# Three edits in one kernel: attention queries computed in full-width tiles, one more projection by seven products, and attention token sums moved from GpSimd to VectorE

## What is computed

```python
c_q = rms_norm(u_mla[..., :Q_LORA], q_g)
q = jnp.einsum('blr,rf->blf', c_q, w_uq).reshape(B, L, MLA_HEADS, QK_DIM)   # 384 -> 8 x 96
q = jnp.concatenate([q[..., :QK_NOPE], rope_axial(q[..., QK_NOPE:], *rot)], axis=-1)
k, v = mla_keys_values(u_mla, kv_g, w_ukv, rot)                             # 256 -> 8 x (64 + 64)
o = block_attention(q, jnp.concatenate([k, kc], axis=1), jnp.concatenate([v, vc], axis=1))
```

```python
cnv = silu(layer_norm(causal_depthwise_conv(a * sigmoid(g)), ln_g, ln_b))   # 31 taps, 1024 channels
merged = (g_attn * (attn @ w_o_attn) + g_rnn * (rnn @ w_o_rnn) + g_conv * (cnv @ w_o_conv))
h = h + merged @ w_out
h = h + (silu(f @ w_ffn_gate) * (f @ w_ffn_up)) @ w_ffn_down
```

## Time and profile before

| | us |
|---|---|
| time, median of 3 runs | 1744.97 |
| lowest and highest of the 3 | 1736.07, 1745.1 |
| the profiled execution's own time | 1739.31 |
| its span on the core | 1737.5 |
| TensorE busy in it | 1675.0 (96%) |
| VectorE busy | 1147.8 (66%) |
| ScalarE busy | 552.7 (32%) |
| GpSimd busy | 661.8 (38%) |

### The profile page before, as it was taken

The page is one execution under the profiler, slowest core; times in us unless marked ns, Lnnn a source line. Parts: engine busy times, 40 slices in busy tenths (PEclk is TensorE's granted clock), DMA queues, the critical chain, the costliest instruction groups (busy, mean ns, idle before and its releaser), DMA issues.

```text
span 1737.5 us, 35985 instructions
## 1 busy us (share of the span) xinstructions
PE 1675.0 (96%) x14722; PEld 1480.8 (85%) x14722; DVE 1147.8 (66%) x2044; ACT 552.7 (32%) x1244; POOL 661.8 (38%) x581
## 2 busy tenths in 40 slices
PE   6999988999999999999999999999999998999999
PEld 3777646888889888878989999989888888999999
DVE  5646155665368789787757664368788896676643
ACT  3232363443343453433330010233554304120100
POOL 1535003554035122115645554164123046445652
PEclk9999996999999999999999999999999999999999
DMA  9333100000443444324344444443343343444543
GB/s 371 137 112 115 65 1 2 5 4 5 182 160 122 146 146 146 122 101 142 124 143 173 168 164 158 164 146 128 120 169 127 137 145 107 162 170 170 170 158 110
DMA packets 53379, 225.71 MB, mean 130 GB/s; under 512 B 5088, under 2 KB 29024, under 8 KB 29280
## 3 DMA queue, kind: packets, MB, share of 16 engines
q1 hardware_dynamic: 53216, 223.40, 36.8%
HBM read 222.34 MB, written 1.05 MB: 129 GB/s over the span
## 4 chain that ended last, share of the span: by engine, by line
PE 87%; DVE 6%; ACT 3%; DMA 1%; issue 1%; DVEq 1%; POOL 0%; SPq 0%; ACTq 0%
PE PS L783 18%; PE PS L740 16%; PE PS L1048 15%; PE PS L1072 8%; PE PS L2531 5%; PE PS L2643 3%; PE PS L2060 2%; PE PS L2073 2%; DVE arena L1455 2%; DMA ring<-stream_dram 1%; PE PS L722 1%; PE PS L2736 1%; PE PS L900 1%; PE PS L863 1%; PE PS L1012 1%
## 5 line engine op out<-in xcount | busy, mean ns | idle before, releaser
L783 PE MATMUL PS<-arena,ring 128*128 128x272 f32 (+1 forms) x1664 | 390.0, 389 | 0.3 <-DVE arena L1683 0.3
L783 PEld LDWEIGHTS PS<-arena,ring 128*128 128x128 f32 x1664 | 311.7, 190 | 59.7 <-issue 6.1
L1455 DVE SCALAR_TENSOR_TENSOR arena<-arena,par 128x272 f32<-128x272 f32 (+1 forms) x480 | 259.5, 599 | 7.4 <-issue 0.9
L1895 POOL TENSOR_TENSOR arena<-ring 128x512 f32<-128x512 f32 x48 | 68.7, 1431 | 443.8 <-DMA ring<-stream_dram 353.9
L740 PE MATMUL PS<-arena,ring 128*128 128x136 f32 (+1 forms) x1536 | 202.0, 280 | 1.4 <-ACT arena L1158 1.4
L740 PEld LDWEIGHTS PS<-arena,ring 128*128 128x128 f32 x1536 | 192.7, 191 | 8.1 <-ACT arena L1158 1.7
L740 PE MATMUL PS<-arena 128*128 128x136 f32 (+1 forms) x1152 | 147.9, 280 | 4.5 <-ACT arena L1138 3.0
L1048 PE MATMUL PS<-arena 128*128 128x136 f32 (+1 forms) x1280 | 152.1, 277 | 0.0
L1048 PEld LDWEIGHTS PS<-arena 128*128 128x128 f32 x1280 | 148.7, 191 | 0.0
L740 PEld LDWEIGHTS PS<-arena 128*128 128x128 f32 x1152 | 140.0, 191 | 5.8 <-POOL arena L1895 1.7
L1048 PE MATMUL PS<-arena,ring 128*128 128x136 f32 (+1 forms) x960 | 116.1, 277 | 0.0
(11 more groups left out here) (417 smaller groups left out, 2966.3 us busy)
## 6 DMA issues: line engine op xcount, KB each, us to landing
ring<-stream_dram SPq DMA_DIRECT2D x185, 1024.0 KB, 4.9
ring<-stream_dram SPq DMA_DIRECT2D x32, 512.0 KB, 4.0
ring<-stream_dram SPq DMA_DIRECT2D x16, 384.0 KB, 3.8
arena<-x_dram SPq DMA_DIRECT2D x1, 2048.0 KB, 8.3
cst<-const_dram SPq DMA_DIRECT2D x1, 1080.0 KB, 7.0
out_dram<-H SPq DMA_DIRECT2D x4, 256.0 KB, 3.1
cst<-const_dram SPq DMA_DIRECT2D x1, 912.0 KB, 12.7
arena<-stream_dram SPq DMA_DIRECT2D x1, 512.0 KB, 11.1
```

Of the source, the lines that this page charges most:

```text
L783: last = mm(PS[:, 2 * (j % 2) + f, nw], w[:, k, P * f:P * f + P], src[:, k, nw], start=k == 0, stop=k == KD - 1)
L1455: stt(CVG[:, c, NQ], CVA[:, c, j + Q0:j + T2], dw_w[l][:, c, j:j + 1], CVG[:, c, NQ], ALU.mult, ALU.add)
L1895: g.tensor_tensor(to[:, 0], w21, w22, ALU.add).then_inc(L["summed"], 1)
```

## The change

1. **Queries.** The 24 matmuls of 96 columns become 18 of 128 columns. A weight tile then holds one head and a third, and a PSUM bank holds tile i of both halves of the heads. ScalarE takes the heads apart by nine copies of 32, 64 or 96 partitions. The rotation's swaps move behind the keys. They write four different groups of 32 partitions of one bank, VectorE multiplies all of it at once, and ScalarE carries the product to the partitions of the queries. The gate rows move into the attention loop, behind its fourth score.
2. **Step 12** joins `MIXED`. The turning of the values moves from ahead of step 13 into its middle.
3. **Attention token sums** move from GpSimd (step 38) to VectorE (step 35 in the first layer, 33 in the second).
4. **Convolution.** `CONV_STEPS` becomes a list for each layer with work moved earlier; layer norm starts at step 36 in the first layer and stays at 37 in the second. The squares and the silu are split in two halves of four tiles, with copies between them.
5. ScalarE's gains (`gain`) of the merge are done between the copies of the next step.

```diff
-CONV_SUM_J = 37
+CONV_SUM_J, ATT_SUM_J = (36, 37), (35, 33)
-MIXED = [*range(2, 8), 9, 11, 15, ...
+MIXED = [*range(2, 8), 9, 11, 12, 15, ...
-              19: 4, ... 25: 1, 26: 1, 27: 4, 28: 5, 29: 3, 30: 5, 31: 5, 32: 3, 33: 4, 34: 4, 35: 5, 36: 1}
+               19: 4, 20: 3, 21: 4, 22: 3, 23: 3, 24: 4, 25: 1, 26: 1, **late}
+              for late in ({27: 4, 28: 8, 29: 3, 30: 7, 31: 5, 32: 3, 33: 4, 34: 4, 35: 1},
+                           {27: 5, 28: 5, 29: 6, 30: 8, 31: 6, 32: 4, 33: 3, 34: 2})]
...
 (VectorE)
+                if j == ATT_SUM_J[l]:
+                    dve.wait_ge(L["o_kept"], B["o_kept"] + len(R))
+                    x = AT.rearrange("p (k e) t -> p k e t", e=2)
+                    token_sums(v, x[:, :, 0], x[:, :, 1], TATT, n0, n1).then_inc(L["att_halves"], 1)
 (GpSimd)
-                if j == OA_J:
-                    pool.wait_ge(L["o_kept"], B["o_kept"] + len(rounds(l)))
-                    front_halves(pairs(AT), TATT, n0, n1, L["att_halves"])
-                    back_halves(pairs(AT), TATT, n0, n1, L["att_halves"])
 (ScalarE, in a mixed step)
                     copy_a(j)
+                    if j == CONV_SUM_J[l] + 1:
+                        square(0)
+                    if j == CONV_SUM_J[l] + 4:
+                        conv_silu(1).then_inc(L["conv_out"], 1)
...
                     copy_g(j)
+                    if j == CONV_SUM_J[l] + 1:
+                        square(1).then_inc(L["conv_sq"], 1)
                     copy_c(j)
 (TensorE, MLA)
-            for h in range(8):
-                if h >= 4:
-                    pe.wait_ge(mq_kept, h - 3)
-                for k in range(3):
-                    w = weights(UQ + h // 4, 3, 384)
-                    last = mm(PS[0:96, h % 4, 0:TX], w[:, k, 96 * (h % 4):96 * (h % 4) + 96], REST[:, 4 + k, :], ...
+            for i in range(3):
+                for g in range(2):
+                    w = weights(UQ + g, 3, 384)
+                    for k in range(3):
+                        last = mm(PS[:, i, TX * g:TX * g + TX], w[:, k, P * i:P * i + P], REST[:, 4 + k, :], ...
+                last.then_inc(mq_made, 1)
...
+            for i in range(4):
+                last = mm(PS[32 * i:32 * i + 32, 4, :], perm32[64:96, :],
+                          QM[64:96, 2 * i:2 * i + 2, :].rearrange("p h t -> p (h t)"), start=True, stop=True)
+            last.then_inc(swap_made, 1)
 (VectorE, MLA)
+            tt(TURNED.rearrange("p (h t) -> p h t", h=2), PS[:, 4, :]..., over(msin, 2), ALU.mult).then_inc(lat_normed, 1)
+            tt(QM[r, :, :], QM[r, :, :], over(mcos[r], 8), ALU.mult)
+            dve.wait_ge(lat_root, 2)
+            tt(QM[r, :, :], QM[r, :, :], PM[r, :, :]..., ALU.add).then_inc(roped, 1)
```

More of the change, by code:

```diff
@@ L215, in build @@
         KR = USH[:, 0, :]
+        TURNED = cut(37120, 512)
         LSQ, LSK = cut(28928, 3, TX), cut(29696, 2, T1)
@@ L1261, in keep_gates, with square, conv_silu, gain @@
                       ).then_inc(L["ga_kept"], 1)
-            def gain(j):
-                for k in (2 * (j - WO_J), 2 * (j - WO_J) + 1):
+            def square(i):
+                act.wait_ge(L["conv_cent"], B["conv_cent"] + 1)
+                return a(CSQ[:, 4 * i:4 * i + 4, NQ], CVG[:, 4 * i:4 * i + 4, NQ], ACT.Square)
+            def conv_silu(i):
+                act.wait_ge(L["conv_normed"], B["conv_normed"] + 1)
+                for k in range(4 * i, 4 * i + 4):
+                    last = a(CVG[:, k, NQ], CVG[:, k, NQ], ACT.Silu, bias=q2l["ln_b"][:, k:k + 1],
+                             scale=q2l["ln_g"][:, k:k + 1])
+                return last
+            def gain(j, tiles=(0, 1)):
+                for k in (2 * (j - WO_J) + f for f in tiles):
                     act.wait_ge(L["mixed"], B["mixed"] + k + 1)
@@ L1280, in scalar_layers @@
                         keep_d(j - 1)
+                    if j >= WO_J + 2:
+                        gain(j - 2, (1,))
                 else:
@@ L2648, in _ @@
             pe.wait_ge(tile_kept, plain_made(27))
-            for i in range(KD):
-                last = mm(PS[:, 7, 2 * i:2 * i + 2], ROWSG[:, i // 2, P * (i % 2):P * (i % 2) + P], SEL, start=True, stop=True)
-            last.then_inc(gate_rows, 1)
             pe.wait_ge(lat_normed, 1)
@@ L2676, in _ @@
                     pe.wait_ge(mk_kept, h - 2)
+                else:
+                    pe.wait_ge(mq_kept, 2 + h // 2)
                 for k in range(2):
@@ L2704, in _ @@
                        start=True, stop=True).then_inc(ms_made, 1)
+                if i == 3:
+                    pe.wait_ge(vt_kept, 4)
+                    for f in range(KD):
+                        last = mm(PS[:, 7, 2 * f:2 * f + 2], ROWSG[:, f // 2, P * (f % 2):P * (f % 2) + P], SEL,
+                                  start=True, stop=True)
+                    last.then_inc(gate_rows, 1)
                 if i >= 3:
@@ L2879, in _, with keep_queries @@
                     a(MT1[:, 0, 0:TX], MT1[:, 0, 0:TX], ACT.Exp, scale=-0.5).then_inc(lat_root, 1)
-            for h in range(8):
-                act.wait_ge(mq_made, h + 1)
-                a(QM[0:96, h, :], PS[0:96, h % 4, 0:TX], ACT.Copy).then_inc(mq_kept, 1)
+            def keep_queries(i, to, of, first):
+                return a(QM[to, first::4, :], PS[of, i, :].rearrange("p (g t) -> p g t", g=2), ACT.Copy)
+            quad = [slice(32 * i, 32 * i + 32) for i in range(4)]
+            act.wait_ge(mq_made, 1)
+            keep_queries(0, slice(0, 96), slice(0, 96), 0)
+            keep_queries(0, quad[0], quad[3], 1).then_inc(mq_kept, 1)
+            act.wait_ge(mq_made, 2)
+            keep_queries(1, quad[1], quad[0], 1)
+            keep_queries(1, quad[2], quad[1], 1)
+            keep_queries(1, halves(0), halves(1), 2).then_inc(mq_kept, 1)
+            act.wait_ge(mq_made, 3)
+            keep_queries(2, quad[2], quad[0], 2)
+            keep_queries(2, quad[0], quad[1], 3)
+            keep_queries(2, quad[1], quad[2], 3)
+            keep_queries(2, quad[2], quad[3], 3).then_inc(mq_kept, 1)
             for h in range(8):
@@ L2885, in _ @@
                 a(KM[0:64, h, :], PS[halves(h % 2), h % 4, :], ACT.Copy).then_inc(mk_kept, 1)
+            act.wait_ge(lat_normed, 2)
+            for i in range(4):
+                last = a(PM[64:96, i, :], TURNED[quad[i], :], ACT.Copy)
+            last.then_inc(lat_root, 1)
             for t in range(4):
@@ L3119, in _ @@
             dve.wait_ge(swap_made, 2)
[L3120 to L3126 removed]
+            tt(TURNED.rearrange("p (h t) -> p h t", h=2), PS[:, 4, :].rearrange("p (h t) -> p h t", h=2), over(msin, 2),
+               ALU.mult).then_inc(lat_normed, 1)
+            tt(QM[r, :, :], QM[r, :, :], over(mcos[r], 8), ALU.mult)
+            dr()
+            dve.wait_ge(lat_root, 2)
+            tt(QM[r, :, :], QM[r, :, :], PM[r, :, :].rearrange("p i (h t) -> p (i h) t", h=2), ALU.add).then_inc(roped, 1)
             for i in range(17):
```

94 lines of the change are left out of this document (37 added, 57 removed).

## The result

The changed kernel took 1717.4 us, the median of 4 runs (1715.66 to 1720.2). The kernel before took 1744.57, the median of 4 (1736.07 to 1745.1). The ratio is 0.9857, 95% interval 0.9824 to 0.989. A second comparison, beside the experiments, gave 0.9885 (0.9865 to 0.9905), from 1717.92 against 1738.77. The medians are 27.2 us apart in the first comparison and 20.9 in the second, and the forecast of 1719 (1708 to 1731) held. The profiled execution's span went from 1737.5 to 1716.4, so 21.1 us less, where the sum said 20.05. All executions were in the same, fast state.

What follows compares the result with a forecast made beforehand. TensorE was taken to bound the kernel, at 87% of its chain of waits. Gains of 6.8, 2.35, 3.4 and 7.5 us sum to 20.05, from 1739.31 to 1719 us, range 1708 to 1731.

Steps and rivals of the forecast that it cites:

- Queries, 6.8 forecast: MLA part: hidden gate rows 1.95, full-width query tiles 2.6, earlier keys 2.4, less 0.2; gain 6.8 us, bounds 2.1 and 7.5.
- The choice between 0.9 and 3.6: MLA part: four swaps take 0.9 us if they overlap; the rival, swaps one after another, 3.6, total 1722, chance 0.12.
- Step 12, 2.35 forecast: Both layers: mixing step 12 saves 0.65 each, and step 13's waits of 0.65 and 0.40 go; gain 2.35 us.
- up to 1.6 a layer: Step 12: the cost in each layer if VectorE's lateness beside GpSimd's weight sums is not covered; costed at nothing.
- the cover: Around step 12: VectorE idles 2.41 us ahead, then waits for ScalarE's roots; nobody waits for it until mid step 13.
- eighth: Step 12: if GpSimd's four sums fully block VectorE, the loss is about an eighth more than the share taken.
- Layer one, 3.4 forecast: Layer one, convolution's norm: waits and slow matmuls of 5.4 us, less 2.0 kept back; gain 3.4, bounds 1 and 5.4.
- the 1.5 that I kept: Layer one: 1.5 us of waits expected to remain, for the halved silu and VectorE's token sums `TCNV`.
- Layer two, 7.5 forecast: Layer two: idleness and slow matmuls of 11.9 us, less 4.4 expected to remain; gain 7.5, bounds 3.5 and 10.
- the relief of 7.0: Layer two: VectorE comes 7.0 us earlier to the norm's first sum, more than the pause of 6.09 there.
- 2.8 for GpSimd's drag: Layer two: some 2.8 us by which GpSimd's token sums slowed VectorE's taps, saved by moving those sums to VectorE.
- 0.8 for the silu, 2.3 for `TCNV`: Layer two: waits expected to remain, 0.8 us for the silu and 2.3 for VectorE's convolution token sums.

Runs made afterwards that it cites:

- e4: Changed kernel with the four swaps writing one group of output partitions in four banks and the old VectorE rotation; ratio 0.989 to the kernel before.
- e9: Changed kernel with the gate rows ahead of the queries and the turn of the values ahead of step 13 again; ratio 0.9937 to the kernel before.
- e2: Kernel before with only step 12 mixed and the turn of the values moved inside step 13; ratio 0.9998 to the kernel before.
- e6: Changed kernel with the old convolution step lists in both layers and the norm at step 37 in both; ratio 0.9915 to the kernel before.
- e5: Changed kernel with the attention token sums back on GpSimd; median 1722.39 us, ratio 0.9897 to the kernel before.
- e7: Changed kernel with ScalarE's squares, silu and gains each in one piece, behind their step's copies; ratio 0.9875 to the kernel before.
- the repeat: The changed kernel run once more without any edit; 1717.92 us, ratio 0.9885 to the kernel before.

## Why the prediction was right, and where its steps were not

**Queries, 6.8 forecast, 6.6 measured.** Each row came as worked out: 8.05 for the queries (7.85), a wait of 0.6 for copies (0.7), 0.99 for the swaps (0.9). The choice between 0.9 and 3.6 rested on the earlier trace rows, and e4 shows that it hangs on the four output groups, not on the place. Gate rows: 1.78 by e9 (1.95).

**Step 12, 2.35 forecast, 1.1 + 1.3 measured** (e2: 1.46 and 1.29). Right in sum, and e9 shows that the wait which the step would have made without the moved turn, 3.46 and 2.96, was never priced: I had taken the 0.65 and 0.40 of the earlier trace rows for it, and the "up to 1.6 a layer" without the cover is 4.9 and 4.8. The "eighth" by which a full block would exceed my share doesn't come out of the rows either: at a share of 0.75 it is a third, which the cover holds as well. The cover chosen (3.67 and two products) was enough for either.

**Layer one, 3.4 forecast, 3.2 measured.** The pause of 2.56 and the slower stretch behind it went, and 1.48 + 0.61 + 0.32 came for the 1.5 that I kept. The reason that I gave, squares within step 37, isn't the only one that suffices: e6 keeps step 37 for the first sum and has no pause either. The token sums back on GpSimd (e5) change nothing in layer one, the old list with the later norm is 0.9 us better (e6), and squares, silu and gains unsplit are 1.2 better (e7). So none of the three is needed there as long as the other two stay. Which of them alone takes the pause away wasn't tried, and the cause in layer one stays open to that extent.

**Layer two, 7.5 forecast, 6.8 and in the repeat 8.0 measured.** The size is right, the reason only half, and that the errors evened out is luck. I made the relief of 7.0 of 6.0 less for VectorE to do, 1.8 of new lateness, and 2.8 for GpSimd's drag. The runs show both: with the new lists the place of the token sums is worth 6.2 (e5), with the new place the lists are worth 4.2 (e6). That 2.8 is the term that was mis-sized. I took half of the 5.7 us for GpSimd's token sums, but they are four of the six operations beside those taps, and with the new lists all eight operations would have stood beside twelve taps and cost 8.2. With the old lists the move takes the pause from 6.09 to 3.75 (e6; step 12 leaves it at 6.09, e2), although it adds 2.8 of VectorE's own work. And the gates, which I had feared from moved steps and put at 1.3, cost 0.49 and 0.26; with the sums on GpSimd the first of them costs 4.98 (e5). Of what I kept back (0.8 for the silu, 2.3 for `TCNV`), 0.69 and 2.40 were measured, and the lower clock behind the latter came once and once not.

**The split of ScalarE's work** carried part of both layer terms in the forecast. By e7 it is worth nothing in sum. `gain` was priced at nothing, and a wait of TensorE behind it shrinks by 0.3 us in each layer.

**The level.** I set 1725 for the median beside 1719 for the profile, and that was 8 us too high: the first three runs of before happened to lie at 1744.97, and 46 later ones gave medians of 1738.5 to 1740.3. The cut was right, the base wasn't. The cut was also helped by chance: 2.3 of the profiled 21.1 us are the scan's clock, which no term had.

## What to carry to other kernels

A wait taken out at one engine's queue is often due next at another's a few microseconds on; order the queue by who needs each result first, and check the next bracket, before splitting work or adding speed. A helper engine that runs ahead of its step puts its work where the waits let it, not where the code has it, so look at what lies beside it in the trace. Compare kernels by stretches cut at the same instructions, not by spans, when one part of the program changes speed from run to run.

## What the hardware showed that I had not expected

- TensorE's granted clock in the scan, a stretch of some 5200 short matmuls with pauses, differs between executions of the same work: means of 0.90 to 0.99, by how long it was at 1.2 in place of 2.4 GHz, and 245.4 to 263.2 us. In e2 it was 1.00 up to 433 us, fell some 2 us behind a pause of 1.09 us, and was still 0.50 between 440 and 450 with TensorE busy throughout. After a pause of 2.4 us in layer two it fell in one execution (3.52 us for 16 matmuls) and not in the other (2.02), with the same code; in e4 and e9, which have that code as well, the 16 took 3.14 and 2.69.
- GpSimd's sums beside VectorE's taps cost VectorE 0.75 to 0.77 us for each of their own. The two take turns, one tap for each sum, 1.42 us apart in place of 0.42.
- Four matmuls of 32 columns that read the same 32 partitions overlap when they write four different groups of 32 partitions (0.99 us), and not when they write one (3.56).
